# Hybrid decoder step on one core: the next head's turns, norms and row sums placed beside the last solve steps of the head before

## The reference

```python
q = l2norm(q) * K ** -0.5;  k = l2norm(k)
decay = exp(where(tril, Gc[:, None] - Gc[None, :], -inf))
Amat = where(strict, (kb @ k.T) * decay, 0)
T = triangular_solve(eye + Amat, eye)
u = T @ (v * beta);  wk = T @ (kb * exp(Gc))
attn = (q @ k.T) * decay;  qg = q * exp(Gc);  k_end = k * exp(g_last - Gc)
# scan over chunks: v_new = u - wk S; o = qg S + attn v_new; S = S exp(g_last) + k_end.T v_new
```

## Time and profile before

| | |
|---|---|
| median of 3 runs | 1435.92 us (1431.0 to 1438.08) |
| the profiled execution: its own time, its span | 1437.64 us, 1435.8 us |
| PE busy | 1335.1 us, 93% |
| DVE, ACT, POOL busy | 51%, 46%, 29% |
| mean granted clock of PE | 0.975 |

### The profile page before, as it was taken

How to read it: one execution, slowest core, us unless ns; L and a number is a source line. 1 busy time by engine, 2 the same in 40 slices (tenths; PEclk the granted TensorE clock), 3 DMA queues, 4 the chain that set the end, 5 groups by cost and what they waited for, 6 DMA issues and landing times.

```text
span 1435.8 us, 26145 instructions
## 1 busy us (share of the span) xinstructions
PE 1335.1 (93%) x10599; PEld 1292.9 (90%) x10599; DVE 727.2 (51%) x1277; ACT 664.3 (46%) x1298; POOL 421.3 (29%) x426
## 2 busy tenths in 40 slices
PE   7999999899999899998989899999999899997995
PEld 7899989779888899998989899999999899997995
DVE  7845444420666343647373743343333667765553
ACT  7564466422433345454454545454533544354453
POOL 0000010002444353736364644545330211212112
PEclk9999999899999999999999999999999999998998
DMA  7224542253111123232423121222222366766563
GB/s 282 65 96 140 155 162 60 59 165 100 60 45 45 59 60 104 76 103 74 135 60 120 55 95 60 62 74 62 73 61 76 94 244 216 244 202 190 181 179 101
DMA packets 48407, 161.27 MB, mean 112 GB/s; under 512 B 5296, under 2 KB 10832, under 8 KB 48032
## 3 DMA queue, kind: packets, MB, share of 16 engines
q1 hardware_dynamic: 39344, 130.77, 29.2%
q10 hardware_dynamic: 8832, 28.33, 5.6%
q0 software_dynamic: 112, 0.50, 0.1%
HBM read 144.32 MB, written 15.26 MB: 111 GB/s over the span
## 4 chain that ended last, share of the span: by engine, by line
PE 75%; DVE 9%; ACT 7%; issue 4%; POOL 3%; DMA 1%; ACTq 0%; SPq 0%; DVEq 0%; POOLq 0%
PE ps L891 38%; PE ps L1200 15%; PE ps L784 11%; PE ps L848 2%; PE ps L852 2%; ACT g_e L1432 1%; PE ps L1168 1%; ACT w_hi L1230 1%; PE ps L1150 1%; POOL w_lo L2109 1%; DVE fin L2097 1%; DVE conv_a L1680 1%; ACT L1436 1%; DVE conv_a L1799 1%; POOL g_e L2174 1%
## 5 line engine op out<-in xcount | busy, mean ns | idle before, releaser
L891 PE MATMUL ps<-h_hi,w_hi 128*128 128x260 f32 x1856 | 412.9, 304 | 31.3 <-POOL w_lo L2109 15.7
L1230 ACT ACTIVATE w_hi<-w_raw 128x512 fp32r<-128x512 f32 x424 | 255.7, 625 | 306.8 <-PE ps L891 160.1
L891 PE MATMUL ps<-h_lo,w_hi 128*128 128x260 f32 x1856 | 380.2, 287 | 0.0
L891 PE MATMUL ps<-h_hi,w_lo 128*128 128x260 f32 x1856 | 379.9, 287 | 0.0
L891 PEld LDWEIGHTS ps<-h_hi,w_hi 128*128 128x128 f32 x1856 | 294.5, 194 | 43.6 <-issue 37.8
L2109 POOL TENSOR_TENSOR w_lo<-w_raw,w_hi 128x512 fp32r<-128x512 f32 x156 | 207.8, 1336 | 353.2 <-ACT w_hi L1230 353.2
L891 PEld LDWEIGHTS ps<-h_hi,w_lo 128*128 128x128 f32 x1856 | 293.3, 193 | 0.0
L891 PEld LDWEIGHTS ps<-h_lo,w_hi 128*128 128x128 f32 x1856 | 293.3, 193 | 0.0
L1641 DVE TENSOR_TENSOR w_lo<-w_raw,w_hi 128x512 fp32r<-128x512 f32 x268 | 184.4, 709 | 147.4 <-ACT w_hi L1230 145.8
L1200 PE MATMUL ps<-y_hi,w_hi 128*128 128x260 f32 x640 | 186.0, 291 | 10.7 <-DVE w_lo L1641 4.3
L1200 PE MATMUL ps<-y_lo,w_hi 128*128 128x260 f32 x640 | 183.9, 287 | 0.0
(11 more groups left out here) (372 smaller groups left out, 1940.8 us busy)
## 6 DMA issues: line engine op xcount, KB each, us to landing
w_raw<-in_w_in SPq DMA_DIRECT2D x120, 512.0 KB, 3.6
w_raw<-in_w_out SPq DMA_DIRECT2D x80, 512.0 KB, 3.8
w_raw<-in_w_mem SPq DMA_DIRECT2D x16, 512.0 KB, 3.6
x_t<-in_x_t SPq DMA_DIRECT2D x8, 520.0 KB, 9.7
fin<-in_x_t SPq DMA_DIRECT2D x8, 520.0 KB, 5.9
out_y_t<-fin SPq DMA_DIRECT2D x16, 260.0 KB, 2.3
c_kv<-in_c_k ACTq DMA_DIRECT2D x8, 512.0 KB, 4.9
c_kv<-in_c_v ACTq DMA_DIRECT2D x8, 512.0 KB, 4.3
```

The source lines that it names most:

```text
L891: last = mm(out[:, hf, :], w, a[:, kk, HALF * hf:HALF * hf + HALF], start=(kk == 0 and j == 0), stop=(kk == KT - 1 and j == 2))
L1230: A(w_hi_of(g)[:, s], raw[:, g % NRAW, s], ACT.Copy).then_inc(sem("w_hi_done"), 1)
```

## The change

Step 0 of a head shrinks to the turns of k and q (PE) and the squares and Ln (ACT), and stands some slots behind step 16 of the head before. DVE's four row operations become an item `gdnrow`, behind step 18 of the head before. So the stage of a head now has its own steps 1 to 19. The turns of v follow the rows in step 1; the small Exps go into ACT's step 1 behind `g_qg`; v is scaled in DVE's step 1, k in step 2. The gram products go to the banks that held the rows (`side[2]`, `side[3]`), and k stays in `side[0]` until it is scaled. The squares' unused outputs go to `g_r1` and `g_kend` of the next head. The state loads and decays of the decode part (`decssdl`, `decssd`) move some slots ahead, and a state load also waits for the reductions of the state two before.

```diff
-STEP_SLOTS = {0: 5, 1: 4, 2: 4, 17: 4, 19: 2}
+STEP_SLOTS = {0: 5, 1: 4, 2: 4, 3: 4, 16: 4, 17: 4}
...
-            extra[0] = [("decssd", a)]
...
         if h <= 3:
-            extra[17] = [("decssdl", 2 * h)]
-            extra[19] = [("decssdl", 2 * h + 1)]
-        steps = []
-        for s in range(CARRY):
+            extra[13] = extra.get(13, []) + [("decssdl", 2 * h)]
+            extra[17] = [("decssdl", 2 * h + 1)]
+            extra[19] = [("decssd", 2 * h)]
+        if h + 1 < GDN_H:
+            extra[16] = [("gdn", h + 1, 0)]
+            extra[18] = [("gdnrow", h + 1)]
+        steps = [("gdn", 0, 0)] + [PAUSE] * 4 + [("gdnrow", 0), PAUSE] if h == 0 else []
+        for s in range(1, CARRY):
...
@@ PE, step 0 @@
-                    pe.wait_ge(*upto("conv_out", N_SSD_T + 3 * (h + 1)))
+                    pe.wait_ge(*upto("conv_out", N_SSD_T + 3 * h + 2))
...
-                        pe.wait_ge(*upto("g_ttf", h))
+                        pe.wait_ge(*upto("g_k_scaled", 2 * h))
+                        pe.wait_ge(*upto("g_t_new", 6 * (h - 1) + 1))
...
-                    for c in range(NC):
-                        last = turn(quad(side[1])[:, c, :], v[:, chunk(c)], ident)
@@ PE, step 1, behind the rows @@
+                    pe.wait_ge(*upto("conv_out", N_SSD_T + 3 * (h + 1)))
+                    if h:
+                        pe.wait_ge(*upto("g_ttf", h))
+                    for c in range(NC):
+                        last = turn(quad(side[1])[:, c, :], v[:, chunk(c)], ident)
+                    last.then_inc(sem("g_vt"), 1)
@@ PE, step 2 @@
-                    pe.wait_ge(*upto("g_scaled", 3 * (h + 1)))
+                    pe.wait_ge(*upto("g_sub", 2 * h + 2))
                     for c in range(NC):
-                        one(quad(side[0])[:, c, :], kk_[:, chunk(c)], kk_[:, chunk(c)])
+                        one(quad(side[2])[:, c, :], kk_[:, chunk(c)], kk_[:, chunk(c)])
+                    pe.wait_ge(*upto("g_qrow", h + 1))
                     for c in range(NC):
-                        last = one(quad(side[1])[:, c, :], kk_[:, chunk(c)], q[:, chunk(c)])
+                        last = one(quad(side[3])[:, c, :], kk_[:, chunk(c)], q[:, chunk(c)])
...
@@ ACT, slot_load @@
                 act.wait_ge(sem(f"out_sst{i % 2}"), 16 * (i // 2))
+                act.wait_ge(*upto("d_yred", 8 * (i - 1)))
@@ ACT, step 0 @@
-                    act.wait_ge(*upto("g_row", h + 1))
-                    A(g_s[:, 3, 0:4], g_row[:, 0, :], ACT.Exp).then_inc(sem("g_ea"), 1)
-                    act.wait_ge(*upto("g_colt", h + 1))
-                    A(g_s[:, 4, 0:4], g_s[:, 4, 0:4], ACT.Exp).then_inc(sem("g_ke"), 1)
@@ ACT, step 1, behind g_qg @@
+                    if h:
+                        act.wait_ge(*upto("g_k_scaled", 2 * h))
+                    A(g_s[:, 3, 0:4], g_row[:, 0, :], ACT.Exp).then_inc(sem("g_ea"), 1)
+                    act.wait_ge(*upto("g_colt", h + 1))
+                    A(g_s[:, 4, 0:4], g_s[:, 4, 0:4], ACT.Exp).then_inc(sem("g_ke"), 1)
...
@@ DVE, step 0 becomes gdnrow (row operations) and is else shared out @@
-                    V.tensor_tensor(g_r1[h % 2][:, :, :], quad(side[1]), along(beta[:, 0:NC, h], P), ALU.mult).then_inc(sem("g_scaled"), 1)
...
@@ DVE, step 1, behind the subtractions @@
+                    dve.wait_ge(*upto("g_vt", h + 1))
...
+                    V.tensor_tensor(g_r1[h % 2][:, :, :], quad(side[1]), along(beta[:, 0:NC, h], P), ALU.mult).then_inc(sem("g_v_scaled"), 1)
...
@@ DVE, step 2, behind g_attn: k is scaled twice (g_r2, g_kend) @@
```

More of the change, by code:

```diff
@@ L967, in _ @@
                     for c in range(NC):
-                        turn(quad(side[2])[:, c, :], q[:, chunk(c)], ident)
-                    for c in range(NC):
-                        last = turn(quad(side[1])[:, c, :], v[:, chunk(c)], ident)
+                        last = turn(quad(side[2])[:, c, :], q[:, chunk(c)], ident)
                     last.then_inc(sem("g_turned"), 1)
@@ L992, in _ @@
                     for c in range(NC):
-                        last = one(quad(side[0])[:, c, :], g_natm[0][:, c, :], ident_r[:, :])
+                        last = one(quad(side[2])[:, c, :], g_natm[0][:, c, :], ident_r[:, :])
                     last.then_inc(sem("g_t0_ps"), 1)
@@ L1002, in _ @@
                             pe.wait_ge(*upto("g_attn", h + 1))
+                            pe.wait_ge(*upto("g_v_scaled", h + 1))
                         for c in range(NC):
@@ L1009, in _ @@
                         if level == 1:
[L1010 to L1011 removed]
+                            pe.wait_ge(*upto("g_attn", h + 1))
                         else:
@@ L1050, in _ @@
                             if h + 1 < GDN_H:
+                                pe.wait_ge(*upto("g_k_scaled", 2 * (h + 2)))
                                 pe.wait_ge(*upto("g_t_new", 6 * (h + 1) + 1))
@@ L1425, in _ @@
                         act.wait_ge(*upto("out_pssd", 16))
-                    else:
-                        act.wait_ge(*upto("g_res", h))
+                    elif h >= 2:
+                        act.wait_ge(*upto("g_o_ps", 4 * (h - 1)))
                     act.wait_ge(*upto("g_turned", h + 1))
-                    for i, (e, bank) in enumerate(((g_e1, side[2]), (g_e2, side[0]))):
+                    for i, (e, bank) in enumerate(((g_r1[h % 2], side[2]), (g_kend[h % 2], side[0]))):
                         for c in range(NC):
@@ L1874, in _ @@
                 gc = SSD_H + GDN_H + h
[L1875 to L1895 removed]
+                if s == 1:
                     dve.wait_ge(*upto("g_rows", h + 1))
@@ L1903, in _ @@
                     dve.wait_ge(*upto("g_exp", 2 * h + 1))
-                    V.scalar_tensor_tensor(flat4(g_natf), side[0], -1.0, flat4(g_e1), ALU.mult, ALU.mult).then_inc(sem("g_nat"), 1)
+                    V.scalar_tensor_tensor(flat4(g_natf), side[2], -1.0, flat4(g_e1), ALU.mult, ALU.mult).then_inc(sem("g_nat"), 1)
                     dve.wait_ge(*upto("g_exp", 2 * h + 2))
-                    V.tensor_tensor(g_attn[h % 2][:, :, :], quad(side[1]), g_e2[:, :, :], ALU.mult).then_inc(sem("g_attn"), 1)
+                    V.tensor_tensor(g_attn[h % 2][:, :, :], quad(side[3]), g_e2[:, :, :], ALU.mult).then_inc(sem("g_attn"), 1)
+                    if h:
+                        dve.wait_ge(*upto("g_wt_ps", h))
+                    dve.wait_ge(*upto("g_ea", h + 1))
+                    V.tensor_tensor(g_r2[:, :, :], quad(side[0]), along(g_s[:, 3, 0:4], P), ALU.mult).then_inc(sem("g_k_scaled"), 1)
+                    dve.wait_ge(*upto("g_ke", h + 1))
+                    V.tensor_tensor(g_kend[h % 2][:, :, :], quad(side[0]), along(g_s[:, 4, 0:4], P), ALU.mult).then_inc(sem("g_k_scaled"), 1)
                 elif s == 3:
@@ L1911, in _ @@
                     dve.wait_ge(*upto("g_t0_ps", h + 1))
-                    V.tensor_tensor(g_t[:, :, :], quad(side[0]), across(ident, NC), ALU.add).then_inc(sem("g_t_new"), 1)
+                    V.tensor_tensor(g_t[:, :, :], quad(side[2]), across(ident, NC), ALU.add).then_inc(sem("g_t_new"), 1)
                 elif 4 <= s < 16 and s % 2 == 0:
```

45 lines of the change are left out of this document (20 added, 25 removed).

## The result

The changed kernel takes 1415.44 us (median of four runs, 1414.85 to 1416.81) against 1433.46 for the kernel before, run beside it (1430.53 to 1438.08): a ratio of 0.9864 with a 95% interval of 0.9838 to 0.9889. It is faster by 1.4%, 18.0 us where 13.9 were forecast (1422 against 1435.92); the time lies inside the range of 1411 to 1431. The profiled execution took 1415.74 us (span 1413.9), 21.9 less than the profiled one before.

A forecast was written before the change was run, and what follows sets the result against it. PE was taken to bound the kernel; its waits in the heads fall from 33.4 to 20.4 us, gain 13.0, plus 1.7 for one slow spell: 1437.64 - 14.7 = 1422.9, forecast 1422 between that and 1421.2, range 1411 to 1431.

The forecast's parts named there:

- what bounds it: Whole kernel: PE is busy 1335.1 of 1435.8 us, so a change pays only where it shortens a PE wait.
- what is late next: Heads 1 to 7: the `w_lo` wait stays behind ACT's Exp step and Silu, 2.16 us each, 15.1 against 15.7.
- R: End of the rows product on PE, from which the prediction counted the chain to `w_lo`; PE goes on at R + 8.70.
- the `g_row` wait: PE's wait for the rows from DVE: goes for heads 1 to 7, 6.5 of the 8.5 us.
- the rival at ACT's queue at the end of a head: Squares and Ln ahead of both `w_hi` pieces make PE wait seven times; slower, about 1445; chance 0.04.
- 0.15 + 1.12 + 0.04 - 0.72 = 0.6 us, five times: 3.0: PE's wait for `g_natm`: start after PE's release, its duration, 0.04, less one k-step; 3.0 us against 8.0.
- which is the main reason for the gain here: `g_natm` wait: the state decay on POOL no longer stands between `w_lo` and the masks; 3.0 us against 8.0.
- Head 0 and the rest: Head 0: row wait 0.7 and 1.0 between gram and first solve product, 1.7 us; `g_p` left at 0.6.
- the three waits named in the last paragraph of the prediction: PE's waits for `g_row`, `w_lo` and `g_natm`; wrong if their sum does not fall by 11 to 17 us.
- I take one spell fewer: Slow clock in the heads: four spells before, one fewer with shorter clusters of waits, 1.7 us gained.
- the clock follows the waits: Rival: one cluster of waits per head sets no clock down, the other three spells go too: 1417; chance 0.13.
- that rival: A table load behind a 512-column Exp waits for ACT to run empty, 18 us over seven heads: 1440; chance 0.01.

The follow-up runs named there:

- experiment 1: Changed kernel with both `w_hi` pieces of the next half unit made at k-step 0 in the first tile of heads 1 to 7: 1397.05 us.
- experiment 8: Changed kernel with the post item holding the Silu swapped ahead of step 1 in heads 1 to 7: 1398.12 us.
- experiment 9: Changed kernel with the two small Exps of ACT's step 1 put ahead of `g_qg`: 1399.14 us.
- experiment 11: Changed kernel with one more 512-column Copy on ACT ahead of `g_qg` in each head: 1423.91 us.
- experiment 4: Kernel before with only the state moves (loads, first decay, added wait), norms, rows and banks as before: 1426.27 us.
- experiment 5: Changed kernel with the first state decay of heads 1 to 4 put right ahead of step 1, all else in place: 1417.98 us.
- experiment 6: Changed kernel with all state moves undone (decay, loads and added wait): 1418.72 us.

## Why the prediction was right, and where it was off

**Right: what bounds it, and what is late next.** The wait on `w_lo` was worked out as 2.16 us in seven heads, 15.1; it measured 15.0. That the sums agree so closely is luck: the waits were 2.30 or 2.31 in four heads and 1.93 or 1.94 in three. The chain itself held: in head 2 `w_hi` was put at R + 6.54 and starts at R + 6.35 (638.97; the rows end at 630.67 + 1.95 = 632.62), PE was let go at R + 8.97 for R + 8.70 and had done 6.67 us of its own work for 6.54. In heads 1 to 4 `w_lo` took 1.77 us instead of 1.32, near a bound of the prediction (1.74); in heads 5 to 7 it took 1.27. The first term, 0.10 from R to the subtraction, does not stand in the earlier trace rows, where the rows end at 868.82 and the subtraction starts at 870.67 behind other work of DVE; it measured 0.03. Experiments 1, 8 and 9 cut the chain at its end, middle and start and experiment 11 lengthened it, and each time PE's waits followed, on `w_lo` or on the next link.

**Right: the `g_row` wait.** Gone in heads 1 to 7, 0.62 us in head 0 where 0.7 was forecast. No wait at k-step 0 of a head's first tile: the rival at ACT's queue at the end of a head did not occur.

**Mis-sized: `g_natm`.** The step "0.15 + 1.12 + 0.04 - 0.72 = 0.6 us, five times: 3.0" measured 0.21 or 0.22 in heads 1 to 4 and none that the view lists in 5 to 7; with 0.70 in head 0 the whole is 1.6. Two terms were off. `g_natm` starts at 641.54, 0.05 ahead of PE and not 0.15 behind it. And PE's k-step was taken from start to start; the view counts a wait from the end of the last matmul, and PE was busy from 641.59 to 642.54, 0.95 us. With 1.16 for the first `g_natm` and 0.05 to PE the sum is -0.05 + 1.16 + 0.05 - 0.95 = 0.21.

**Wrong: "which is the main reason for the gain here"**, said of the state decay. In the kernel before the state moves alone remove all 8.0 us of `g_natm`'s wait (experiment 4). In the changed kernel it is not: with the decay back ahead of the masks the wait is the same 1.5 us, 18.3 in all (experiments 5 and 6). The trace of before showed where POOL stood; it could not show that the norm move removes the same wait by itself.

**Head 0 and the rest.** 1.7 was forecast, 0.62 + 0.70 + 1.16 = 2.5 measured: the wait behind the gram was sized well (1.16 for 1.0), that for `g_natm` in head 0 was left out. `g_p`, left alone at 0.6, went. Together 18.4 of waits instead of 20.4: against the 33.4 of the prediction a gain of 15.0 for the forecast 13.0, and 15.7 with `g_res`, whose four waits of at most 0.2 us it left out; the three waits named in the last paragraph of the prediction fell from 32.2 to 17.2, within its 11 to 17.

**Wrong in sign: the clock.** "I take one spell fewer" was five instead of four, 3.4 us worse than forecast. The reason given, shorter clusters, does not hold: each head has fewer waits, but the one left is as long as those after which the clock had fallen before. The rival "the clock follows the waits" had the spells go with the waits that the change removes; they went only when the last long one did. In the six kernels whose longest wait in heads 1 to 7 is 0.74 us or less, none is left in the heads, 8.5 us less than in the change.

**What made up for it.** Of the 21.9 us between the profiled runs, 17.1 lie in the stage of the heads (from the end of the scan part, 487.4 and 485.1, to the first output product, 1139.5 and 1120.0), 2.3 ahead of it and 2.4 behind it. In the two outer parts one slow spell fewer each, 1.7, makes most of it, and the change touches nothing there: these 4.7 us were not forecast, and that they fell to the changed kernel's side is luck. In the heads 15.7 - 1.7 = 14.0 is accounted for; the other 3.1 us is shorter busy time of PE for the same 5065 matmuls of that stage (612.7 to 611.2, although the second holds a spell more). Whether these are restarts after waits that no longer occur was not separated.

**The load that follows an Exp.** The load at 637.17 stands right behind a 512-column Exp that ends at 636.54 + 0.62 = 637.16: 0.01 us. From there to the start of the Silu at 638.47 it is 1.31 us. The Trainium skill (ScalarE: Activation LUTs, What ACT_TABLE_LOAD costs) adds a drain of 1.38 us to each switch, 2.66 in all; this trace does not agree, and the chance of 0.01 for that rival was fair. What a switch costs here is its 1.28 us, if it stands in a chain: two stood in this one, and experiments 8 and 9 each took one out of it.

## What to carry to other kernels

When a wait of the critical engine has been worked out as a chain of another engine's queue, look for an item in that chain that something late doesn't need: swapping two neighbours in one queue (the Silu and the Exp step, or the small Exps and the large one) gave nearly as much again as the whole rearrangement (17.3 and 16.3 us for 18.0). Take parts of a change out of the changed kernel as well as putting them into the old one, since two parts may each remove the same wait. And where positions come from dealing a list out evenly, compare the order after an edit: one more entry shifted its neighbours and gave a result that belonged to the shift.

## What the runs showed that was not expected

**A wait of about 2 us often goes with a slow spell, which costs 1.7 us more.** In the change four of the seven waits of 1.93 to 2.31 us were followed by slow spells, five in all; with the Copy added six of the seven of 2.31 to 3.02, seven in all; where no wait after head 0 exceeds 0.74 there is none. Most spells start behind the end of the wait, a few up to 0.9 us ahead of it. It is not the length alone: the same 2.31 us in head 1 left the clock at 1.00 in the change and was followed by a spell with the Copy added, and the two waits of 3.2 us in heads 5 and 6 stood with none in the kernel before and with one each in experiment 4. What decides it stays open.

**POOL's `w_lo` took longer beside one DVE operation than beside another.** In heads 1 to 4 it took 1.77 us while DVE made the z gate's product (L1826, both sources in SBUF, at 639.58). In head 5 the same operation took 1.27 us while DVE scaled k out of PSUM (timeline of the changed kernel, as above):

```profile
853.19 1.27 POOL L2124 TENSOR_TENSOR w_lo<-w_raw,w_hi 128x512 fp32r<-128x512 f32 x1 [4.95 <-ACT w_hi L1241]
...
853.21 0.68 DVE L1906 TENSOR_TENSOR g_r<-ps,g_s 128x512 f32<-128x512 f32 x1
...
854.40 0.74 DVE L1826 SCALAR_TENSOR_TENSOR y_raw<-conv_a,vecs,y_raw 128x512 f32<-128x512 f32 x1
854.56 1.61 POOL L2206 TENSOR_TENSOR g_natm<-g_natf,masks 128x512 fp32r<-128x512 f32 x1
```

There `g_natm` fell beside L1826, and took 1.61 us where it had 1.12 in the earlier trace rows and 1.16 in head 2 of this kernel. That the place of the sources decides was not tried by itself.
